# Attention scores from split fp32r operands, a later weighing, and a closing LayerNorm read from PSUM

## The reference, cut to what matters

```
x = first_block(x, ...)                       # untouched by the change
h = layernorm([meta tokens (16), x])          # L = 528 rows
z = h @ w_in -> q_a, kv_a, k_pe, q_g, k_g, v_g
# MLA, 4 heads: 128 columns without position ("nope") and 64 with ("rope")
q_m = [q_nope, rotate(q_rope)];  k_m = [kv_nope, rotate(k_pe), the same for all heads]
# GQA, 4 query heads on 2 key heads, 128 columns, all rotated after an RMS norm
o   = softmax(q k^T * scale) v                # per head, 528 keys
h   = layernorm(sqrt(2) h + [rms(o_mla), rms(o_gqa)] @ w_o)
h   = layernorm(sqrt(2) h + experts(h))       # 32 experts, 4 per token
return h[16:]                                 # 512 rows
```

## Time and profile before

| | |
|---|---|
| median of 3 runs | 2024.15 us (2023.11 to 2026.75) |
| the profiled execution | 2020.8 us, span 2019.0 us |
| busy, share of the span | PE 1959.0 us (97%), DVE 1695.8 (84%), ACT 1366.6 (68%), POOL 384.3 (19%) |
| granted TensorE clock, mean | 0.984 |

### The profile page before, as it was taken

One profiled execution on the slowest core, in us unless ns is written; L12 is line 12 of the kernel. 1 busy time (PEld: TensorE's weight loads), 2 busy tenths in 40 slices (PEclk: granted clock), 3 DMA queues, 4 the chain that ended last, 5 costly groups with the idle time before them and its releaser, 6 DMA issues.

```text
span 2019.0 us, 29369 instructions
## 1 busy us (share of the span) xinstructions
PE 1959.0 (97%) x8740; PEld 1541.8 (76%) x8740; DVE 1695.8 (84%) x1726; ACT 1366.6 (68%) x1734; POOL 384.3 (19%) x335
## 2 busy tenths in 40 slices
PE   4999999998999999999999999999999999999997
PEld 2657767786767787888888888888888888888885
DVE  6899977349744479999999999999999999999997
ACT  3456855224355526888888888888888888888885
POOL 6571000000000108211111111111111221112110
PEclk7999999999999988999999999999999999999999
DMA  7222235332010257999999999999999999999994
GB/s 295 96 104 84 84 104 178 116 99 79 22 63 1 64 167 268 380 394 363 365 381 366 380 361 375 377 368 387 363 371 376 361 378 365 375 373 364 375 362 178
DMA packets 149007, 533.04 MB, mean 264 GB/s; under 512 B 14351, under 2 KB 19631, under 8 KB 145184
## 3 DMA queue, kind: packets, MB, share of 16 engines
q1 hardware_dynamic: 132912, 492.45, 65.0%
q0 software_dynamic: 16048, 39.99, 7.7%
HBM read 517.75 MB, written 24.26 MB: 268 GB/s over the span
## 4 chain that ended last, share of the span: by engine, by line
PE 88%; DVE 6%; ACT 3%; DMA 2%; issue 1%; SPq 0%; DVEq 0%; ACTq 0%
PE ps L920 50%; PE ps L1036 4%; PE ps L1084 4%; PE ps L1029 4%; PE ps L858 3%; PE ps L1132 3%; PE ps L827 2%; PE ps L1065 2%; PE ps L1041 2%; PE ps L1260 2%; PE ps L945 2%; ACT arena L1712 1%; DVE arena L2359 1%; ACT arena L1710 1%; DVE arena L2353 1%; DMA ring<-in_mod_w 1%
## 5 line engine op out<-in xcount | busy, mean ns | idle before, releaser
L920 PE MATMUL ps<-split,xTs 128*128 128x512 f32 x3264 | 771.3, 392 | 0.7 <-ACT split L1704 0.5
L920 PEld LDWEIGHTS ps<-split,xTs 128*128 128x128 f32 x3264 | 611.3, 188 | 130.9 <-ACT split L1704 1.2
L2340 DVE TENSOR_TENSOR split<-arena,split 128x2048 fp32r<-128x2048 f32 x204 | 466.6, 2287 | 42.7 <-ACT split L1704 42.7
L2340 DVE TENSOR_TENSOR split<-ring,split 128x2048 fp32r<-128x2048 f32 x204 | 469.0, 2318 | 20.0 <-ACT split L1704 20.0
L1704 ACT ACTIVATE split<-arena 128x1024 fp32r<-128x1024 f32 x408 | 409.7, 1054 | 97.7 <-PE ps L920 95.3
L1704 ACT ACTIVATE split<-ring 128x1024 fp32r<-128x1024 f32 x408 | 410.3, 1055 | 93.0 <-PE ps L920 56.9
L920 PE MATMUL ps<-split,aTs 128*128 128x512 f32 x1632 | 385.4, 392 | 0.0
L920 PEld LDWEIGHTS ps<-split,aTs 128*128 128x128 f32 x1632 | 303.8, 188 | 62.6 <-DVE split L2340 0.4
L1826 DVE TENSOR_TENSOR split<-ring,split 128x2048 fp32r<-128x2048 f32 (+1 forms) x32 | 72.6, 2270 | 66.4 <-ACT split L1371 66.4
L725 POOL DMA_INDIRECT y_rows<-arena,slots x33 | 71.0, 2152 | 268.7 <-issue 250.4
L736 POOL DMA_DIRECT2D slots<-slot_rows x66 | 54.8, 831 | 328.0 <-issue 328.0
(11 more groups left out here) (412 smaller groups left out, 2481.5 us busy)
## 6 DMA issues: line engine op xcount, KB each, us to landing
ring<-in_w_gate_up SPq DMA_DIRECT2D x170, 1024.0 KB
arena<-in_w_gate_up SPq DMA_DIRECT2D x102, 1024.0 KB
arena<-in_w_down SPq DMA_DIRECT2D x102, 1024.0 KB
ring<-in_w_down SPq DMA_DIRECT2D x34, 1024.0 KB
ring<-in_w_in SPq DMA_DIRECT2D x24, 1024.0 KB
ring<-in_mod_w SPq DMA_DIRECT2D x12, 1024.0 KB
ring<-in_w_out SPq DMA_DIRECT2D x8, 1024.0 KB
ring<-in_pw_w SPq DMA_DIRECT2D x4, 1024.0 KB
```

The costliest lines, as they stand in the source:

```text
L920: m = mm(ps[:, banks + q, :], lhs[:, x_, k, :], w[:, q * 512:(q + 1) * 512], start=start, stop=stop)
L2340: V.tensor_tensor(split[:, 1, s_, :].rearrange("p a b -> p (a b)"), chunk_pair(p), split[:, 0, s_, :].rearrange("p a b -> p (a b)"), ALU.s ...
```

## The change

Three things are changed together.

1. The scores are made of fp32r products. Each of `qnT`, `knT`, `qgT`, `kgT`, `krT`, `qpT` becomes a pair, the high part copied by ACT as before and a low part that DVE subtracts (PSUM minus high, counted by the semaphore `qk_lo`). A GQA score is three products per half of the keys; an MLA score is three nope products and two rope products, for which the rotated queries are written twice (rows 0 to 63 and 64 to 127) and their second copy is turned into the low part, so that high and low stand on one 128-row operand. PE waits for `qk_lo` where it waited for `turned` or `qkn` before it writes a bank again, and before the first scores.
2. `weigh(u-1)` stands after `turn(u)`, ahead of `scores(u+2)`.
3. At the end, the last item's rows are split into `y_last[0]` (ACT) and `y_last[1]` (DVE) and added by fp32r one-hot products; DVE subtracts the mean and multiplies by the gain in one pass from PSUM; ACT multiplies by rstd; GpSimd adds the bias of tiles 0 to 2; DVE closes the last tile by halves.

```diff
 # PE, attention
-                    for dst, kk in keys:
-                        if hh < HM:
-                            mm(dst, qnT[:, hh, q], knT[:, hh, kk], start=True, stop=False)
-                        else:
-                            i = mm(dst, qgT[:, hh - HM, q], kgT[:, (hh - HM) // 2, kk], start=True, stop=True)
-                    for dst, kk in keys:
-                        if hh < HM:
-                            pb = ROPE * (hh % 2)
-                            i = mm(dst, qpT[pb:pb + ROPE, hh // 2, q], krT[pb:pb + ROPE, kk], start=False, stop=True)
+                    for x_, w_ in ((0, 0), (0, 1), (1, 0)):
+                        for dst, kk in keys:
+                            i = mm(dst, mine[0][x_], mine[1][w_][:, kk], start=((x_, w_) == (0, 0)), stop=(hh >= HM and x_ == 1))
+                    if hh < HM:
...
+                        for kr in (krT, krT_lo):
+                            for dst, kk in keys:
+                                i = mm(dst, part[:, j // 2, j % 2, :], kr[:, kk], start=False, stop=(kr is krT_lo))
...
-                pe.wait_ge(sig("qkn"), 2 * HM + 1)
-                pe.wait_ge(sig("qpT"), TC)
+                pe.wait_ge(sig("qk_lo"), LO_END)
                 scores(0)
                 scores(1)
                 for u in range(len(UNITS)):
                     turn(u)
+                    if u >= 1:
+                        weigh(u - 1)
...
                     if u + 2 < len(UNITS):
                         scores(u + 2)
-                    weigh(u)
+                weigh(len(UNITS) - 1)
 # PE, turns of rotated tiles
                 if o >= 1:
-                    pe.wait_ge(sig("turned"), o)
+                    pe.wait_ge(sig("qk_lo"), o)
...
-                if t >= 1:
-                    pe.wait_ge(sig("turned"), first + t)
+                if n_ == 4 and t >= 1:
+                    pe.wait_ge(sig("qk_lo"), LO_B + t)
+                if n_ == 2 and t >= 2:
+                    pe.wait_ge(sig("qk_lo"), LO_C[t - 2] + 1)
...
-                for j in range(2):
-                    i = nc.tensor.transpose(ps[:, BANK_QN[t % 2], j * P:(j + 1) * P], qrot[:, t, j * P:(j + 1) * P], IDENT)
+                pe.wait_ge(sig("vm"), t + 1)
+                for j in range(HM):
+                    i = nc.tensor.transpose(ps[:, BANK_QN[t], j * P:(j + 1) * P], qrot[:, t % 2, j * P:(j + 1) * P], IDENT)
 # DVE, low parts
+            def lo_of(low_, ps_, high_):
+                V.tensor_tensor(low_, ps_, high_, ALU.subtract).then_inc(sig("qk_lo"), 1)
...
             z_sums(LC)
+            kr_low(3)
             z_sums(LC + 1)
+            kr_low(4)
             rotate_b(0)
...
             z_sums(LC + 3)
+            weights_low(W_Z + 5)
+            qg_low(0)
             rotate_b(2)
-            weights_low(W_Z + 5)
+            qg_low(1)
             rotate_b(3)
+            qg_low(2)
...
+            for j in range(HM):
+                qn_low(j)
+            rotate_c(LC - 1)
             for t in range(TC):
...
+                kg_low(t)
+                kn_low(t)
+                if t in (1, 2):
+                    rotate_qp(t - 1)
+            kg_low(TC)
...
+            rotate_qp(2)
+            qp_low(0)
+            rotate_qp(3)
+            for t in range(1, TC):
+                qp_low(t)
 # DVE, the end
+            wait_alone(dve, sig("y_ready"), n_items + 1)
+            V.scalar_tensor_tensor(y_last[1], ps[:, 4:6, :].rearrange("p a b -> p (a b)"), gate_s[:], y_last[0], ALU.mult, ALU.subtract).then_inc(sig("y_ready"), 1)
...
             def last_gain(t):
+                sums = ps[:, SUM_BANK[t]:SUM_BANK[t] + 2, :].rearrange("p a b -> p (a b)")
                 dve.wait_ge(sig("ln_var"), TC + t + 1)
...
+                V.scalar_tensor_tensor(ybuf[t], sums, bn_mv[:, t, 0:1], ln_rows[:, 0, :], ALU.subtract, ALU.mult).then_inc(sig("ln2_vec"), 1)
+
             for t in range(TC):
...
+                last_stats(t)
+                last_gain(t)
...
+                V.scalar_tensor_tensor(x[:, c_], x[:, c_], ln_rstd[:, TC - 1:TC], ln_rows[:, 1, c_], ALU.mult, ALU.add).then_inc(sig("ln2_vec"), 1)
 # ACT, the end
+                A(ybuf[t], ybuf[t], ACT.Copy, scale=ln_rstd[:, t:t + 1]).then_inc(sig("ln2_normed"), 1)
 # POOL, the end
+            for t in range(TC - 1):
+                pool.wait_ge(sig("ln2_normed"), t + 1)
+                nc.gpsimd.tensor_tensor(ybuf[t], ybuf[t], ln_rows[:, 1, :], ALU.add).then_inc(sig("out_ready"), 1)
```

More of the change, by code:

```diff
@@ L152, in program @@
         R_FROM, R_TO = 2048, 27552
+        with nc.sbuf_tensor("arena_k", [P, HM * L], F32R) as arena_k:
+            pass
+        with nc.sbuf_tensor("arena_to_g", [P, R_TO], F32):
+            with nc.sbuf_tensor("arena_g", [P, 2 * L], F32R) as arena_g:
+                pass
         with nc.sbuf_tensor("arena_head", [P, R_FROM], F32):
@@ L236, in program @@
         m2 = Area(0)
-        qnT = m2.take(HM, T)
+        squares_at = Area(0)
+        knT_lo = m2.take(HM, L, of=arena_k, base=0)
         rtmp = m2.take(2, 384)
@@ L244, in program @@
         kvanT = m2.take(L)
-        krT = m2.take(L)
-        qpT = m2.take(2, T)
+        krT, krT_lo = m2.take(L, of=arena_r), m2.take(L, of=arena_r)
+        qp2 = m2.take(4, P, of=arena_r)
         AT_H = m2.at
@@ L251, in program @@
         h = m2.take(LC, D)
+        kgT_lo = [Area(m2.at - D + g * L).take(L, of=arena_r) for g in range(2)]
+        m2.take(32)
         after_h = m2.at
         hz = [xTs, aTs, m2.take(2, KD, P, of=arena_r), m2.take(2, KD, P, of=arena_r), hTm]
-        m2.take(2 * P - P)
+        m2.take(P - 48)
         at_z = m2.at
@@ L316, in program @@
         SUM_BANK = (2, 0, 6, 4)
+        y_last = [aTs[:, x, :, :].rearrange("p k n -> p (k n)") for x in range(2)]
+        oh_last = xTs[:, 0, 0:TC, :]
         bgu_raw = Area(at_z + 448 * LC + 512 * TC + 512 * LC + 2 * TILE).take(2 * D)
@@ L409, in program @@
         AT_A, AT_B, AT_C, AT_QP = 0, LC, LC + TC, 2 * LC + TC
+        LO_B, LO_QN = LC, LC + TC
+        LO_C, LO_KN = [LO_QN + HM + 2 * t for t in range(TC)] + [LO_QN + 3 * HM], [LO_QN + HM + 2 * t + 1 for t in range(TC)]
+        LO_QP = LO_QN + 3 * HM + 2
+        LO_END = LO_QP + TC
+        QP_DONE = [2 * HM + 1 + n for n in (1, 2, 3, 5)]
         HALF = L // 2
@@ L1574, in _ @@
                 act.wait_ge(sig("qpT_ps"), t + 1)
-                A(qpT[:, :, t * P:(t + 1) * P], ps[:, BANK_QN[t % 2], 0:256].rearrange("p (h n) -> p h n", h=2), ACT.Copy).then_inc(sig("qpT"), 1)
+                for first, part in qpT[t]:
+                    A(part, rope_ps(t, first, part), ACT.Copy).then_inc(sig("qkn"), 1)
             def probs(u):
@@ L1729, in _, with last_rstd @@
                 split_high(22, 24)
-            output(n_items)
+            act.wait_ge(sig("acc"), 2 * TC)
+            act.wait_ge(sig("lo_used"), n_items * PAIRS + SPLITS // 2)
+            act.wait_ge(sig("slot_s_in"), n_items * 16 + 16)
+            A(y_last[0], ps[:, 4:6, :].rearrange("p a b -> p (a b)"), ACT.Copy, scale=gate_s[:]).then_inc(sig("y_ready"), 1)
             nc.scalar.preload_act_table_set("natural_log_exp_and_others")
-            for t in range(TC):
+            def last_rstd(t):
                 act.wait_ge(sig("ln_var"), TC + t + 1)
@@ L1990, in _ @@
             ss = z_ss.rearrange("p (t s) -> p t s", t=LC)
-            sq_two = [qnT[:, x, :] for x in range(2)]
+            sq_two = [squares_at.take(T) for x in range(2)]
             st.link(V.memset(z_ss, 1.0))
@@ new lines, in kg_low, with qn_low @@
+            def kg_low(t):
+                r = rows_of(t)
+                dve.wait_ge(sig("turned"), AT_C + t + 1)
+                for g in range(2):
+                    i = V.tensor_tensor(kgT_lo[g][:, t * P:t * P + r], ps[:, 2 + t % 2, g * P:g * P + r], kgT[:, g, t * P:t * P + r], ALU.subtract)
+                i.then_inc(sig("qk_lo"), 1)
+            def qn_low(j):
+                dve.wait_ge(sig("qkn"), j + 1)
+                lo_of(qnT_lo[:, j, :], ps[:, BANK_QN[j], :], qnT[:, j, :])
```

155 lines of the change are left out of this document (101 added, 54 removed).

## The result

The changed kernel takes 2011.48 us (median of 4 runs, 2008.84 to 2011.72), the kernel before beside it 2023.63: ratio 0.9941, 95% interval 0.9927 to 0.9956, 12 us less. Forecast were 2011.4 us in a range of 2002 to 2020. The profiled execution has a span of 2009.67 us, 9.35 less than that of before (2019.02); the profiled execution of before, 2020.8 us, was itself about 3 us faster than its median.

The account below looks back on a forecast made before the run. PE was taken to bound projections, attention and experts, DVE mostly the end. Attention -18.8, low parts +9.3, slow clock +1.8 and end -5.0 sum to -12.7, from 2024.15 to 2011.4 us; range 2002 to 2020.

Parts of the forecast that it names:

- The scores: Attention: fp32r scores at 0.122 us a product and the later weighing gain 18.8 us, after start and switching losses.
- the slow start: Around the first scores: PE's waits for DVE lower its clock for one start, +1.8 us (0 to 3.6).
- the weighing's wait on ScalarE: Attention, each unit: weighing's first weight load waits for ScalarE's copy; reordering removes 0.2 us, leaving 2.0 of 2.2.
- The low parts: Before the first scores: DVE's low-half subtractions, 18.0 us of work plus 2.3 of waits after 558.9, delay them by 9.3.
- The turn's 0.9: Projections: PE's third q tile at 535.19 also waits for the previous tile's low part, 0.68 plus 0.2 hand-over.
- its bound of 11: Upper bound of the delay before the first scores: +11 us if each low part also waits 0.1 for its copy.
- a sign of being wrong: Start of attention: first scores before 574 or after 583 us would show the forecast wrong; 579.2 was expected.
- The end: Closing stage: one DVE pass per tile and biases on GpSimd end the kernel at 2014.0 against 2019.0, -5.0 us.
- DVE did not hide the low parts: Rival, projections: PE's products end the stage, which grows some 3 us without the slow start; 2003.3 us, chance 0.12.
- GpSimd did not end the kernel: Rival, closing stage: GpSimd's adds take twice 2.7 us, the end costs +1.5; 2017.9 us, chance 0.13.
- the product is not priced by the instruction: Rival, scores: an fp32r product costs 0.23 us whatever its columns; 2039.2 us, chance 0.06.
- The softmax was not the unit here: Rival, attention: softmax links run serially, units at least 3.4 us, gain 6.8 instead of 18.8; 2023.4 us, chance 0.06.

Follow-up runs that it names:

- the clock held: Changed kernel plus 15 unread f32 products in five PE waits between the last key rotation and the first scores: 2008.87 us, ratio 0.9932.
- the second experiment: Kernel before with only the later weighing, turn(u), weigh(u-1), scores(u+2), scores still f32: 2019.69 us, ratio 0.9985.
- third experiment: Changed kernel with the weighing's old order put back, turn(u), scores(u+2), weigh(u): 2013.87 us, ratio 0.9954.

## Why the prediction was right, step by step

- *The scores.* Column c fell by 17.6, column d rose by 1.2: 16.4 for the attention. Column b, 4.35, holds 1.1 of the slow start (3.27 with the clock held), so without it the attention gained 17.5 where 18.8 were forecast. The price of a product was hit, 0.1225 for 0.122; most units came out as forecast, 2.79 for 2.73 + 0.05 and 3.27 for 3.22 + 0.05.
- *But not by its reasons for the rest of a unit.* Credited were 0.2 in each unit for the weighing's wait on ScalarE. The trace and the second experiment show that the MLA units had no such wait, and that in GQA units its 0.2 came back in the scores behind the weighing. What was gained in its place is the turn, 0.15 faster once it stands behind products of 128 rows: 0.44 with f32 and with fp32r scores of GQA units, 0.59 behind the weighing or behind the 64-row rope products. The MLA scores were worth more than credited, 0.95 a unit with the order put back where 1.97 - 1.22 = 0.75 was counted. Errors met here: the step failed as a mechanism and held as a sum, and that is luck. The 0.2 in the scores was that of 16-row products, which nothing in the forecast had seen.
- *The weighing's real worth* is the wait that the faster scores would have opened, 0.31 in GQA units (third experiment), which the forecast did not have as a term; the last weighing's delay of 1.2 was left out too.
- *The low parts.* The turn's 0.9 stands on the timeline as forecast, DVE's work of 18.0 was 17.4. Its waits were put at 2.3 and were 4.92, so the term came to +11.35 (10.45 in column a and the 0.9) for +9.3, just over its bound of 11. With the clock held the waits are 2.95 and the term is 9.4 (31.19 in column a): the sum of the low parts was right, and what was mis-sized is the price of the slow clock. That was put at 1.8, all of it behind the scores' start; the runs show 2.0 ahead of it, in DVE's waits, and 1.1 in column b. Together 11.1 were forecast, and 12.4 came. In the kernel with the bias on DVE, which is the same code up to here, it was 10.5. The first scores at 583.13 were past the 583 that the forecast named as a sign of being wrong; without the drift of 1.93 it is 581.2.
- *The end.* -5.0 forecast, -4.99 here and by itself. Inside, GpSimd's add was dearer in the forecast (2.7, measured 2.35), and the closing halves cheaper (1.29, measured 2.02, the first of them beside GpSimd). From the first sum to its last instruction DVE gained 5.75 where 6.3 were forecast, and the write behind it grew by 0.7 where 1.3 were: two errors that cancel.
- *The rivals.* DVE did not hide the low parts, GpSimd did not end the kernel, the product is not priced by the instruction (0.1225 for half of the columns at 0.23). The softmax was not the unit here, but is close: it shows in some GQA units as soon as the 16-row gaps go.

The stages of the two traces sum to +0.90 + 10.45 + 0.03 - 17.61 + 1.17 - 1.25 - 4.99 = -11.30, and the drift ahead of them, 1.93, makes it, but for rounding, the -9.35 of the spans. The -1.25 in the experts is not settled: column e varies from 1302.4 to 1304.7 over the executions while their code is the same.

That the median met the forecast to 0.1 us is luck: by stages -12.7 were forecast and -11.3 measured, of which the experts' -1.25 was in no term. And the kernel before, measured again beside the changed kernel and the experiments, has medians of 2021.45 to 2023.63, where the forecast set out from 2024.15.

## What to carry to other kernels

Splitting an operand moves work from the engine that multiplies to the one that subtracts: look at how long the subtracting engine is idle ahead of the point where everything must be ready, since only that much is free. Look at starts of consecutive matmuls, not at the mean of a record: a row count that changes from 128 to 16 and back cost more here than the whole of the reordering gave (7.3 us against 4.7), and padding with zeros took it away. And where PE must wait for some microseconds in several pieces, count the lower clock in the work just behind each wait too.

## What was not expected of the hardware

- A product of 16 rows among those of 128 costs about 0.1 us at each of four steps (0.205, 0.213, 0.200 and 0.227 between starts, 0.112 otherwise); padded to 128 rows an MLA unit is 0.39 us shorter and a GQA unit, where the softmax does not hold it up, 0.34.
- Four turns behind f32 products of 64 rows, or behind the 16-row ones of the weighing, take 0.59 us, behind products of 128 rows 0.44.
- DVE's pass of 512 columns with two SBUF inputs takes 1.35 us when a GpSimd add is at work for its first 0.81, and 0.74 alone; GpSimd's add of 1024 columns takes 2.35 beside it and 2.35 to 2.38 otherwise.
- 15 products that nobody reads, put into PE's waits, held its granted clock at 1.00 in both executions that had them (565 to 585 us); in the eight others with the low parts it was 0.50 to 0.83 from 575 to 585.
